# Two weight units behind six layer norms are multiplied with the unnormalised g*y and repaired afterwards; the sums of two more norms stand ahead of the projections

## What is computed

```python
def layer_norm(x, g, b):
    mu = jnp.mean(xf, -1, keepdims=True)
    var = jnp.mean(jnp.square(xf - mu), -1, keepdims=True)
    return ((xf - mu) * lax.rsqrt(var + EPS) * g + b).astype(x.dtype)
...
        x = layer_norm(DN_ALPHA * x + m, ln1_g[i], ln1_b[i])
        x = layer_norm(DN_ALPHA * x + conv_ffn(x, ...), ln2_g[i], ln2_b[i])
        gate = jax.nn.sigmoid(x @ ple_w_gate[i] + ple_b_gate[i])
        x = x + gate * (p[i] @ ple_w_proj[i])
```

## Time and profile before

| | us |
|---|---|
| median of 3 runs | 1900.05 (1898.75 to 1901.45) |
| time of the profiled execution | 1898.58 |
| its span in the profile | 1896.8 |
| TensorE busy | 1838.8 (97% of the span) |
| VectorE busy | 1153.5 (61%) |
| ScalarE busy | 989.0 (52%) |
| GpSimd busy | 91.0 (5%) |
| DMA | 297.8 MB, 157 GB/s, queues 47% of 16 engines' span |
| mean granted clock of TensorE | 0.996 of full speed |

### The profile page before, as it was taken

The page is one execution under the profiler, slowest core; times in us unless marked ns, Lnnn a source line. Parts: engine busy times, 40 slices in busy tenths (PEclk is TensorE's granted clock), DMA queues, the critical chain, the costliest instruction groups (busy, mean ns, idle before and its releaser), DMA issues.

```text
span 1896.8 us, 33583 instructions
## 1 busy us (share of the span) xinstructions
PE 1838.8 (97%) x14536; PEld 1792.3 (94%) x14536; DVE 1153.5 (61%) x1778; ACT 989.0 (52%) x1564; POOL 91.0 (5%) x88
## 2 busy tenths in 40 slices
PE   8989999999999999999999999999999999899997
PEld 7778999998989999999999999999999999899997
DVE  6655798656367886565555765554545555665554
ACT  5555666556436664654445445443554444664443
POOL 0001100100012001000010020001000001020001
PEclk9999999999999999999999999999999999999999
DMA  5332455545415555455554535555344554235552
GB/s 192 111 112 95 158 188 186 185 142 177 135 47 182 185 183 188 155 168 178 171 174 136 176 134 174 171 178 177 135 148 157 188 185 151 89 121 191 188 184 84
DMA packets 85044, 297.80 MB, mean 157 GB/s; under 512 B 10496, under 2 KB 13440, under 8 KB 84896
## 3 DMA queue, kind: packets, MB, share of 16 engines
q1 hardware_dynamic: 82400, 294.16, 46.8%
q10 hardware_dynamic: 2496, 1.49, 0.3%
HBM read 294.57 MB, written 1.05 MB: 156 GB/s over the span
## 4 chain that ended last, share of the span: by engine, by line
PE 86%; DVE 7%; ACT 3%; POOL 1%; issue 1%; DMA 1%; ACTq 0%; DVEq 0%; POOLq 0%
PE ps L1229 27%; PE ps L1231 27%; PE ps L1230 26%; PE ps L1277 1%; POOL acc L759 1%; DVE w_lo L780 1%; DVE var L814 1%; ACT w_hi L361 1%; ACT x L400 1%; DMA icol<-pos 1%; ACT a_hi L404 1%; PE ps L1273 1%; PE ps L1395 0%; DVE y L808 0%; PE ps L1620 0%
## 5 line engine op out<-in xcount | busy, mean ns | idle before, releaser
L780 DVE TENSOR_TENSOR w_lo<-raw,w_hi 128x1024 fp32r<-128x1024 f32 x557 | 691.4, 1249 | 430.3 <-ACT w_hi L361 303.3
L361 ACT ACTIVATE w_hi<-raw 128x1024 fp32r<-128x1024 f32 x557 | 581.2, 1051 | 188.2 <-DMA raw<-stream 165.0
L1229 PE MATMUL ps<-a_hi,w_hi 128*128 128x256 f32 (+1 forms) x2336 | 665.0, 285 | 11.3 <-DVE w_lo L780 3.7
L1231 PE MATMUL ps<-a_hi,w_lo 128*128 128x256 f32 (+1 forms) x2336 | 662.9, 284 | 0.0
L1230 PE MATMUL ps<-a_lo,w_hi 128*128 128x256 f32 (+1 forms) x2336 | 662.3, 284 | 0.0
L1229 PEld LDWEIGHTS ps<-a_hi,w_hi 128*128 128x128 f32 x2336 | 441.7, 189 | 17.1 <-issue 8.0
L1231 PEld LDWEIGHTS ps<-a_hi,w_lo 128*128 128x128 f32 x2336 | 441.9, 189 | 0.0
L1230 PEld LDWEIGHTS ps<-a_lo,w_hi 128*128 128x128 f32 x2336 | 440.0, 188 | 0.3
L1229 PE MATMUL ps<-h_hi,w_hi 128*128 128x256 f32 (+1 forms) x1376 | 390.0, 283 | 6.4 <-DVE h_lo L1144 3.6
L1231 PE MATMUL ps<-h_hi,w_lo 128*128 128x256 f32 (+1 forms) x1376 | 389.2, 283 | 0.0
L1230 PE MATMUL ps<-h_lo,w_hi 128*128 128x256 f32 (+1 forms) x1376 | 388.8, 283 | 0.0
(11 more groups left out here) (229 smaller groups left out, 1566.8 us busy)
## 6 DMA issues: line engine op xcount, KB each, us to landing
raw<-stream SPq DMA_DIRECT2D x557, 512.0 KB, 3.6
x<-xT SPq DMA_DIRECT2D x1, 1024.0 KB, 7.1
out<-x SPq DMA_DIRECT2D x8, 128.0 KB, 1.7
work<-pT ACTq DMA_DIRECT2D x2, 256.0 KB, 2.6
par<-params ACTq DMA_DIRECT2D x1, 283.5 KB, 4.6
tmp<-causal ACTq DMA_DIRECT2D x1, 208.0 KB, 2.4
con<-consts ACTq DMA_DIRECT2D x1, 194.5 KB, 6.4
tmp<-pos ACTq DMA_DIRECT2D x1, 128.0 KB, 15.1
```

The source lines that it names most:

```text
L361: nc.scalar.activation(w_hi[:, u % SLOTS, :], raw[:, u % SLOTS, :], ACT.Copy).then_inc(w_hi_ready, 1)
L780: nc.vector.tensor_tensor(w_lo[:, u % SLOTS, :], raw[:, u % SLOTS, :], w_hi[:, u % SLOTS, :].bitcast(F32), ALU.subtract).then_inc(w_lo_rea ...
L1229: nc.tensor.matmul(dst, wh, xh, start=first, stop=False, skip_group_check=True)
L1231: return nc.tensor.matmul(dst, wl, xh, start=False, stop=last, skip_group_check=True)
```

## The change

For the norms `mla`, `gla`, `ffn2`, `conv`, `ffn3` and `att`, the first two units of the next product are multiplied with g*y instead of the normalised x. With y unnormalised, W(x) = rstd * W(g*y) - mu * rstd * (W g) + W b. ScalarE splits g*y into `a_hi` and VectorE into `a_lo` (`z_high`, `z_low`) as the tiles of y come; two further columns of the operand hold g and b, so the same matmuls give W g and W b. `z_opening` runs these two units right behind `stats` in banks 4 and 5, and then an `opening` of the next four units on the normalised x, which overwrites the operand tile by tile. `z_fix` on VectorE repairs the two results in PSUM. The repaired units are consumed late: after 10 hidden tiles in feed-forward parts 0 and 1, after 3 in parts 3 and 5, as second group in `conv_in`, at once in `kv_k`. The splits of the three weight units that the longer opening and its successor need stand inside the norm (`hi(ahead + 4..6)`, `lo(ahead + 4..6)`). The 24 idle matmuls of all these norms go.

For `ffn0` and `ffn1`, `stats` stands ahead of both projections, without idle matmuls behind them; the projections have banks 4 to 7, and the gate opens with four units. The root's table is loaded earlier everywhere. `a_hi` and `a_lo` have 274 columns a tile instead of 272.

```diff
+Z_LN = {"mla": "up0", "gla": "up1", "ffn2": "conv_in", "conv": "up3", "ffn3": "kv_k", "att": "up5"}
+Z_LATE = {0: 10, 1: 10, 3: 3, 5: 3}
+Z_BANKS = (4, 5, 0, 1, 2, 3, 6, 7)
+CONV_ORDER = (1, 0, 2, 3, 4, 5, 6, 7)
+TZ = T + 2
...
-        a_hi = sb("a_hi", [P, KD, T], F32R)
-        a_lo = sb("a_lo", [P, KD, T], F32R)
+        a_hi = sb("a_hi", [P, KD, TZ], F32R)
+        a_lo = sb("a_lo", [P, KD, TZ], F32R)
...
+            def z_high(name, tiles, cw):
+                k, z = LN[name], Z_AT[name]
+                for n in tiles:
+                    if n == 0:
+                        nc.scalar.activation(a_hi[:, :, T:TZ], gain_bias(k), ACT.Copy).then_inc(z_hi_ready, 1)
+                    nc.scalar.activation(a_hi[:, n, cw], y[:, n, cw], ACT.Identity,
+                                         scale=pcol("ln_g", KD * k + n)).then_inc(z_hi_ready, 1)
...
+                if ahead is not None:
+                    hi(ahead + 4)
                 act.wait_ge(stats_ready, k + 1)
...
+                if ahead is not None:
+                    hi(ahead + 5)
+                if meanwhile:
+                    meanwhile()
                 for n in range(KD):
                     act.wait_ge(normed, KD * k + n + 1)
...
+                        if name in Z_LN:
+                            if n < KD - 1:
+                                act.wait_ge(z_used, (KD - 1) * Z_AT[name] + n + 1)
+                            else:
+                                act.wait_ge(unit_done, ahead + 2)
...
+            def z_low(name, tiles, cw):
...
+                    dve.wait_ge(z_hi_ready, (KD + 1) * z + n + 2)
+                    nc.vector.scalar_tensor_tensor(a_lo[:, n, cw], y[:, n, cw], pcol("ln_g", KD * k + n),
+                                                   a_hi[:, n, cw].bitcast(F32), ALU.mult, ALU.subtract).then_inc(z_split, 1)
+
+            def z_fix(name, i, dst=None):
...
+                whole = ps[:, 4 + i, 0:n_cols]
+                rest = sq[:, i, cw]
+                dve.wait_ge(unit_done, BASE[Z_LN[name]] + i + 1)
+                link(nc.vector.tensor_copy(z_col[:, i, :], ps[:, 4 + i, n_cols:n_cols + 2]))
+                nc.vector.tensor_scalar(rest, acc1[:, cw], z_col[:, i, 0:1], z_col[:, i, 1:2], ALU.mult, ALU.add).then_inc(dve_step, 1)
+                link(nc.vector.tensor_tensor(whole, whole, var[:, cw], ALU.mult))
+                nc.vector.tensor_tensor(whole if dst is None else dst, whole, rest, ALU.add).then_inc(z_fixed, 1)
+
+            def layer_norm(name, split, ahead=None):
+                if ahead is not None:
+                    lo(ahead + 4)
                 dve.wait_ge(meansq_ready, k + 1)
...
+                    if n == 0 and ahead is not None:
+                        lo(ahead + 5)
                     if n + 2 < KD:
                         less_mean(n + 2)
...
+                if ahead is not None:
+                    lo(ahead + 6)
+                if name in Z_LN:
+                    link(nc.vector.scalar_tensor_tensor(acc1[:, cw], mu[:, cw], -1.0, var[:, cw], ALU.mult, ALU.mult))
...
+                    split = not (f in Z_FFN and i < 3)
...
+                        if split:
+                            lo_next(u)
...
+                    if f in Z_FFN and pos == Z_LATE[f] - 1:
+                        z_fix(Z_FFN[f], 0)
+                        z_fix(Z_FFN[f], 1)
...
+            for rank, n in enumerate(CONV_ORDER):
                 u = BASE["conv_in"] + 3 * n
+                nb = rank % 2
+                if n == 0:
+                    z_fix("ffn2", 0, f_tg[:, nb, :])
+                    z_fix("ffn2", 1)
+                    dve.wait_ge(z_fixed, 2 * Z_AT["ffn2"] + 2)
+                else:
+                    lo_next(u)
...
+                if n >= 2:
+                    lo_next(u + 1)
...
+                if n == 0:
+                    lo_next(u + 4)
+                    lo_next(u + 5)
+                if n >= 2:
+                    lo_next(u + 2)
...
+            def z_opening(name, x_stage):
...
+                pe.wait_ge(w_lo_ready, base + 2)
+                pe.wait_ge(z_split, (KD + 1) * z + 1)
                 for k in range(KD):
+                    pe.wait_ge(z_split, (KD + 1) * z + k + 2)
+                    for i in range(2):
+                        ins = three(ps[:, BANK[base + i], 0:n_cols], *tile(base + i, k), a_hi[:, k, wide_cols],
+                                    a_lo[:, k, wide_cols], k == 0, k == KD - 1)
...
+                opening(phase, cw, a_hi, a_lo, x_split, X_SPLIT[x_stage], 4, 2)
...
+            stats(LN["ffn0"], TOK, 4, 0)
             project(0, 0)
-            stats(LN["ffn0"], TOK, 4, 0)
             project(0, 1)
-            keep_busy(12, (BASE["gate0"] + 3) % BANKS)
-            stream_product("gate0", TOK, a_hi, a_lo, "ln1")
+            gate(0, "ln1")
```

More of the change, by code:

```diff
@@ L67 @@
 CONV_FFNS = (0, 1)
+Z_LN = {"mla": "up0", "gla": "up1", "ffn2": "conv_in", "conv": "up3", "ffn3": "kv_k", "att": "up5"}
+Z_AT = {_name: _i for _i, _name in enumerate(Z_LN)}
+Z_FFN = {0: "mla", 1: "gla", 3: "conv", 5: "att"}
+Z_LATE = {0: 10, 1: 10, 3: 3, 5: 3}
+Z_BANKS = (4, 5, 0, 1, 2, 3, 6, 7)
+CONV_ORDER = (1, 0, 2, 3, 4, 5, 6, 7)
+Z_ORIGIN = {"up0": "up0", "up1": "up1", "conv_in": "conv_in", "conv_out": "conv_in", "up3": "up3",
+            "kv_k": "kv_k", "kv_v": "kv_k", "kv_f": "kv_k", "up4": "kv_k", "up5": "up5"}
+BANK = []
+for _name, _n in PHASES:
+    for _i in range(_n):
+        _u = BASE[_name] + _i
+        if _name in Z_ORIGIN:
+            _u -= BASE[Z_ORIGIN[_name]]
+            BANK.append(Z_BANKS[_u] if _u < 8 else _u % BANKS)
+        elif _name in ("gate0", "gate1"):
+            BANK.append(_i)
+        else:
+            BANK.append(_u % BANKS)
+TZ = T + 2
 ATT_Q_BANK = (0, 1, 2, 0, 1, 0, 1, 0)
@@ L85, with up_order @@
     NCON += _n
+def up_order(f):
+    late = Z_LATE.get(f, 0)
+    return [*range(1, late + 1), 0, *range(late + 1, NF)]
 def ffn_cols(f):
@@ L709, in _ @@
             ffn(4)
[L710 removed]
+            layer_norm("ffn4")
             warm(ACT.Exp)
@@ L937, in ffn @@
                     lo_next(last)
+                    if f"ffn{f}" in Z_LN:
+                        z_low(f"ffn{f}", range(4 * half, 4 * half + 4), cw)
             def head_mask(t):
@@ L1216, in _ @@
             lo_next(u + 3)
+            z_low("att", range(4), TOK)
             for i in range(4, 8):
@@ L1359, in project, with gate, wide @@
                 ins.then_inc(unit_done, 1)
-            def wide(phase, cw, k, h_count):
-                opening(phase, cw, h_hi, h_lo, h_split, h_count - KD, 4)
+            def gate(l, x_stage):
+                opening(f"gate{l}", TOK, a_hi, a_lo, x_split, X_SPLIT[x_stage], 4)
+                for n in range(4, KD):
+                    u = BASE[f"gate{l}"] + n
+                    pe.wait_ge(pp_copied, 4 * l + (2, 2, 3, 4)[n - 4])
+                    whole(TOK, a_hi, a_lo)(u, n, n, n // 2, n % BANKS)
+            def wide(phase, cw, k, h_count, order=range(KD)):
+                opening(phase, cw, h_hi, h_lo, h_split, h_count - KD, 4, 0, order)
                 for i in range(4, 8):
```

353 lines of the change are left out of this document (206 added, 147 removed).

## The result

The changed kernel takes 1902.74 us (median of 20 runs, 1900.25 to 1904.5), the kernel before 1900.0 us (20 runs, 1898.1 to 1901.9). The ratio is 1.0015, 95% interval 1.0008 to 1.0022: 2.7 us slower. That is inside the 0.2% that I called no change, but clear of noise, and outside my range, which ended at 1902; I had forecast 9 us faster. The span of the profiled execution is 1899.7 us against 1896.8.

What follows compares the result with a forecast made beforehand. TensorE's work plus its pauses was taken to bound the kernel. Savings of 21.3 and 3.1 us less 3.3, 3.6, 5.9, 2.1 and 0.55 gave 8.95 us saved, so 1890.5 us, range 1876 to 1902.

Steps and rivals of the forecast that it cites:

- rival C: Longer rows of `a_hi` and `a_lo` slow the matmuls reading them; at 3 ns each 21 us, so 1911 us; chance 0.10.
- Nothing for pauses of 2 us: TensorE pauses of 2 us were taken to cost no clock, so 0 us stood in the sum.
- The term of 1.7 us: In `gla` and `conv`, tiles y wait behind `z_low`, so the pooled sums end some 1.0 and 0.7 us later.
- the Trainium skill's rule: VectorE and GpSimd exclude each other in SBUF: each `z_low` beside the sums holds them 0.42 us, up to 7 us.
- the late stalls of `up0` and `up1`: Two repairs and a pair without weight split make TensorE wait 1.8 us, twice: 3.6 us, bounds 0 and 7.
- the fall behind `conv_in`: After the long pause in `conv_in`, 4 us of work at half clock, counted as 2.1 us lost.
- the saving of norm `mla`: Two units fill the idle hole, second opening starts 2.0 us later, at 217.8: 3.65 us saved.
- the stall behind the opening: In `up0` and `up1` a weight split stands behind the first pair's work; TensorE waits 1.65 us, twice: 3.3 us.
- the one in `conv_in`: Splits stand behind both groups and both repairs, so TensorE stands 5.9 us; bounds 3 and 8 us.
- The gates: In the gates VectorE's chain starts 1.55 us earlier, with one `lo` less; twice, 3.1 us saved.
- Rival A: VectorE's order hides the repairs, most stalls do not come and the clock stays up: about 1879 us; chance 0.22.
- Rival B: Each later start and stall is half as large again, so all is given back: 1898 to 1900 us; chance 0.15.

Runs made afterwards that it cites:

- e1: The kernel before with only the tile rows of `a_hi` and `a_lo` widened from 272 to 274 columns: 1904.59 us, ratio 1.0025.
- e3: The changed kernel with idle matmuls added in the pauses ahead of the second openings and of `up2`: 1899.71 us, ratio 1.0002.
- e10: The changed kernel with `conv_in` taken back to its form before the change, the other five norms keeping their two units: 1899.02 us, ratio 0.9996.
- e11: The kernel before with 16 idle matmuls in place of 24 behind the sums of seven norms: 1906.86 us, ratio 1.0037.
- e6: The changed kernel with the weights of the eighth unit of `up0` and `up1` split at the end of the norm: 1900.27 us, ratio 1.0002.
- e4: The changed kernel with the banks of `conv_in` and `conv_out` turned by one from the ninth unit on: 1900.68 us, ratio 1.0002.

## Why the prediction was wrong

I had 8.95 us saved; between the two profiles 2.98 were lost. Three terms failed, two that I had put at nothing and one that was too small.

- **The rows, 4.7 us.** This was rival C, which I gave 0.10, with its price far too high (3 ns a matmul) and its place too wide: 4968 matmuls of 256 columns got 1.4 ns dearer, 2040 of 272 got 1.1 ns cheaper (4968 x 1.4 - 2040 x 1.1 = 4.7); e1 measured 4.85. Its sign of being wrong, a step above 0.1184 us in the `up` phases, came (0.1197); its break-even of 1.3 ns came true at one width, with the other sign at the other. The step that failed is that nothing of it stood in the sum, on the ground that "nothing in the rows depends on an address": no row had tried another row length, so it was a price with open bounds.
- **The clock, 4.9 us.** "Nothing for pauses of 2 us" failed. Three falls came that I had not counted: 1.50 and 1.78 us (e3), and 1.58 us behind `gla` (`up1` is that much shorter in e10, where nothing in it differs and the clock stays up). e11 shows 6.9 us for such pauses alone. The row that I took for it, 3.0 us nearly idle at clock 1.00, was one execution's luck: behind the same pause e1 and e11 show half clock.
- **The sums, 2.5 us.** The term of 1.7 us (`gla` 1.0, `conv` 0.7, `att` 0) was 4.2. I had the mechanism for two norms, but too small (they took 1.55 and 1.43), and for `att` I missed that four `z_low` stand ahead of the fifth residual. What I had derived from the Trainium skill's rule (18 `z_low` at 0.42 us would be 7.6 us, not the 7 that I wrote) did not come: each add is stretched as the rows show, but GpSimd is busy no longer than before. My sign for it, sums over 1.5 us later, was just met in `gla` (1.55 us) by the late start of the adds.

The other way went smaller items, about 1.7 us: `kv_k` shows no step over 0.33 us behind its second opening, where I had a stall of 0.55; the late stalls of `up0` and `up1` are 0.4 us less than forecast; and of the fall behind `conv_in`, which I priced at 2.1 us, 2.8 us fell into work, an estimate of 1.4 us. That leaves about 1.5 us of the 11.9 between forecast and profile open, most of it in `up3`, which is 0.8 us longer than rows and sums explain. These are phases of two single executions.

What held: the saving of norm `mla` (second opening at 218.09 for 217.8), the stall behind the opening (1.69 for 1.65), the one behind the repairs (1.60 for 1.8), the one in `conv_in` (5.81 for 5.9). The gates gave 1.34 and, without the clock at `up2`, some 1.3 us for 1.55; a part of their 2.1 us came back as a longer wait in the next phase. Rival A did not come. Rival B's 1898 to 1900 was the nearest, but for the wrong reason: the stalls were not larger than forecast, prices that I had set at nothing were. Its own sum is also wrong: the later starts of the six norms come to 13.6 us and the stalls to 12.8, half of both is 13.2 us in place of my 10.5, and the rival would have been at about 1904. That 1898 to 1900 came near is luck.

## What to carry to other kernels

Where a tile gets a new row length, price it as a change to every matmul that reads it, from a run if one can be had: here two columns more cost 4.85 us, more than any one norm gave. Before idle matmuls are taken out, ask what clock they hold, and count each new pause of 2 us or more as a chance of a fall, some 1.5 us here; one profile in which such a pause was borne does not show that it always is. And put a pair's work between two repairs: two side by side cost 3 us here that a change of order gave back.

## What the hardware showed beyond that

- The same pause ends in two ways. Norm `conv`, 2.05 us idle in both: in the changed kernel 24 matmuls in the next 3 us at clock 1.00 (above), in e6, which has nothing changed in this norm and gets there 1.0 us earlier in its trace, 17 at 0.64 (changed kernel, then e6). `up3` is 1.5 us longer for it. The length of a pause didn't decide it alone; the start-up pause above shows the same.

```profile
1148.34 0.36 PE L1367 MATMUL ps<-a_hi,w_hi 128*128 128x272 f32 x1 [2.05 <-DVE a_lo L932]
```

```profile
1147.33 0.36 PE L1371 MATMUL ps<-a_hi,w_hi 128*128 128x272 f32 x1 [2.05 <-DVE a_lo L934]
```

```profile
1147.50:1150.50 3.00, 3.00 (x17) 3.00 (x17) 3.00 (x10) 3.00 (x7) 0.00 (x0) 0.64 0.48 195
```

- Apart from the one at the very end, all half-clock stretches were 3.4 or 6.8 us long, whatever the pause beside them (2.0 to 5.8 us). The same 5.81 us pause in `conv_in` came with 3.4 us in the changed kernel and with 6.8 us in e6, where the phase is 1.0 us longer; the 3.40 us pause of e4 came with 6.8 us.
- The length of a row moves the matmul's step by 1 to 2% with TensorE never idle, and of the four lengths tried the best for 256 columns (1152 bytes) is not that for 272 (1096).
